# The first layer's condition weights in two pieces by output half, and a first feed-forward slot built up in two halves

## The reference, cut to what matters

```python
def _layer(x, c, l, prm, past):
    ada = jax.nn.silu(c) @ prm['w_ada'][l] + prm['b_ada'][l]
    ada = ada.reshape(B, N_SUB, 3, D)[:, :, :, None, :]

    def pre(j, z):
        return _rmsnorm(z, prm['g_pre'][l, j]) * (1 + ada[:, j, 1]) + ada[:, j, 0]

    def post(j, z, y, w):
        return (z + w * (1 + ada[:, j, 2]) * _rmsnorm(y, prm['g_post'][l, j])).astype(z.dtype)

    x = post(0, x, _swiglu(pre(0, x), prm['w_ffn_in'][l, 0], prm['w_ffn_down'][l, 0]), FFN_RES)
    y, st = _mix(pre(1, x), l, prm, past)
    x = post(1, x, y, 1.0)
    x = post(2, x, _swiglu(pre(2, x), prm['w_ffn_in'][l, 1], prm['w_ffn_down'][l, 1]), FFN_RES)
```

## Time and profile before

| | us |
|---|---|
| median of 3 runs | 1829.71 (1825.85 to 1831.72) |
| the profiled execution, its own time | 1823.39 |
| its span, first to last instruction | 1821.5 |
| mean granted TensorE clock in it | 0.978 of 2.4 GHz |
| PE busy | 1735.8 (95%) |
| DVE, ACT busy | 1053.0 (58%), 790.3 (43%) |

### The profile page before, as it was taken

The page is one execution under the profiler, slowest core; times in us unless marked ns, Lnnn a source line. Parts: engine busy times, 40 slices in busy tenths (PEclk is TensorE's granted clock), DMA queues, the critical chain, the costliest instruction groups (busy, mean ns, idle before and its releaser), DMA issues. The chain is left out here.

```text
span 1821.5 us, 33383 instructions
## 1 busy us (share of the span) xinstructions
PE 1735.8 (95%) x12724; PEld 1509.6 (83%) x12724; DVE 1053.0 (58%) x1903; ACT 790.3 (43%) x1428; POOL 67.2 (4%) x99
## 2 busy tenths in 40 slices
PE   5999999999998999999979999999999899989998
PEld 3898978878875687999969889788878667879997
DVE  3554555576567656565455554465665666665653
ACT  2554434345333215555345554344345222255552
POOL 0000000000000000000000000100000000000000
PEclk8999999999998999999999999999999989999999
DMA  8778555546448925555657784664553597355561
GB/s 335 266 268 329 212 219 199 208 163 242 164 164 278 318 93 203 182 174 209 253 195 278 265 336 163 231 242 152 193 203 139 196 329 256 116 203 173 179 220 58
DMA packets 85947, 391.83 MB, mean 215 GB/s; under 512 B 12472, under 2 KB 17856, under 8 KB 55488
## 3 DMA queue, kind: packets, MB, share of 16 engines
q1 hardware_dynamic: 72664, 368.15, 55.6%
q10 hardware_dynamic: 13160, 22.02, 3.4%
HBM read 377.31 MB, written 12.83 MB: 214 GB/s over the span
## 5 line engine op out<-in xcount | busy, mean ns | idle before, releaser
L1100 DVE TENSOR_TENSOR ring_parts<-ring,pages_parts 128x1024 fp32r<-128x1024 f32 (+1 forms) x288 | 334.0, 1193 | 157.6 <-ACT pages_parts L1716 157.5
L567 PE MATMUL ps<-arena_parts,pages_parts 128*128 128x264 f32 x1536 | 395.0, 291 | 18.0 <-DVE xn_parts L1188 10.4
L1716 ACT ACTIVATE pages_parts<-ring 128x1024 fp32r<-128x1024 f32 (+1 forms) x288 | 285.4, 1029 | 178.5 <-DMA ring<-in_w_ffn_in 55.3
L568 PE MATMUL ps<-xn_parts,pages_parts 128*128 128x264 f32 x1408 | 357.5, 288 | 0.0
L567 PEld LDWEIGHTS ps<-arena_parts,pages_parts 128*128 128x128 f32 x1536 | 295.1, 192 | 36.7 <-issue 30.2
L568 PEld LDWEIGHTS ps<-xn_parts,pages_parts 128*128 128x128 f32 x1408 | 269.2, 191 | 0.0
L572 PE MATMUL ps<-arena_parts,ring_parts 128*128 128x264 f32 x1536 | 222.8, 285 | 0.0
L528 PE MATMUL ps<-xn,ring 128*128 128x264 f32 x896 | 208.7, 388 | 0.3 <-ACT xn L1723 0.3
L572 PEld LDWEIGHTS ps<-arena_parts,ring_parts 128*128 128x128 f32 x1536 | 202.4, 190 | 0.0
L528 PEld LDWEIGHTS ps<-xn,ring 128*128 128x128 f32 x896 | 166.7, 190 | 33.8 <-ACT gates L1830 3.5
L567 PE MATMUL ps<-big_parts,pages_parts 128*128 128x264 f32 x704 | 176.0, 285 | 0.0
(11 more groups left out here) (351 smaller groups left out, 2556.5 us busy)
## 6 DMA issues: line engine op xcount, KB each, us to landing
ring<-in_w_ffn_in SPq DMA_DIRECT2D x88, 1024.0 KB, 5.0
ring<-in_w_ada SPq DMA_DIRECT2D x32, 1536.0 KB, 6.7
ring<-in_w_a SPq DMA_DIRECT2D x32, 1536.0 KB, 7.2
ring<-in_w_ffn_down SPq DMA_DIRECT2D x32, 1408.0 KB, 6.1
pages<-in_k_pages SPq DMA_DIRECT2D x128, 256.0 KB, 5.3
pages<-in_v_pages SPq DMA_DIRECT2D x128, 256.0 KB, 4.0
ring<-in_w_ada SPq DMA_DIRECT2D x24, 1024.0 KB, 6.6
ring<-in_w_proj SPq DMA_DIRECT2D x8, 1536.0 KB, 9.7
```

What stands on the lines that cost most here:

```text
L567: mm(ps[:, b, 0:T], tile, hi[:, k, :], start=start, stop=False)
L568: return mm(ps[:, b, 0:T], tile, lo[:, k, :], start=False, stop=False)
L1100: v.tensor_tensor(ring_lo[:, r, at * P:(at + n) * P], w, whi[:, place, 0:n * P].bitcast(F32), ALU.subtract)\
L1716: A(whi[:, place, 0:n * P], ring[:, r, at * P:(at + n) * P], ACT.Copy).then_inc(S.whi_ready, 1)
```

## The change

The eight loads of shift and scale weights become sixteen of half a megabyte. Piece `p` (0 or 1) holds, for both shift and scale, the columns of channel chunks 4p to 4p+3, over all input chunks. They don't go through the ring but into `big`, `gates`, `pj` and `wbuf`, which are free at that time, so that SP needs to wait for nothing: piece 0, then slot 0's feed-forward weights, then piece 1. Of each partition's row of a load, two runs of 512 numbers (2 KB) are read where it was one of 2048 (8 KB).

PE does piece 0, the first half of piece 1 (input chunks 0 to 3), then for chunks 0 to 3 all 24 products of slot 0 (`early_products`), the other half of piece 1, and the 24 products of chunks 4 to 7. DVE and ACT go through tables, modulation and split of the input by piece (`early_columns`, `early_split`); slot 0's weights are split on DVE between the two. Of the constants, only the identity and the ones are loaded at the start. The masks (into `pj`), the other four constants, `sel` and the page table are issued behind the fourth `w_ada12` load; the masks are made into bytes behind feed-forward slot 18. For the first layer the loops of two rounds are written out; the second layer keeps them.

```diff
@@ SP
-                    sp.dma_start(consts[:], ins.consts).then_inc(S.k_in, 16)
+                    sp.dma_start(consts[:, 0:2, :], ins.consts[:, 0:2, :]).then_inc(S.k_in, 16)
                 def late_loads():
-                    sp.dma_start(tt8, ins.masks).then_inc(S.t_in, 16)
+                    sp.dma_start(masks_in, ins.masks).then_inc(S.t_in, 16)
+                    sp.dma_start(consts[:, 2:6, :], ins.consts[:, 2:6, :]).then_inc(S.t_in, 16)
...
+                def load_early(p):
+                    for q in range(QUARTERS):
+                        for g in range(2):
+                            columns = ins.w_ada8[layer, g * QUARTERS + q].rearrange("p (u h c) -> p u h c", u=2, h=EARLY)
+                            sp.dma_start(early_block(p, g, q), columns[:, :, p, :]).then_inc(page_full[p * (1 + q // 2)], 16)
                 if first_layer:
-                    for k in range(8):
-                        load(ins.w_ada8[layer, k], 1)
-                        if k == 3:
-                            late_loads()
+                    load_early(0)
+                    load(ins.w_ffn_in[layer, 0, 0], 2)
+                    load_early(1)
+                    for k in range(16):
+                        if k:
+                            load(ins.w_ffn_in[layer, 0, k], 2)
+                        if k % 2:
+                            load(ins.w_ada12[layer, k // 2], 1)
+                        if k == 7:
+                            late_loads()
@@ PE
+                def early_ada(p, quarters):
+                    if quarters[0] == 0:
+                        adas()
+                        pe.wait_ge(S.ada_row, p + 1)
+                    home = p * (1 + quarters[0] // 2)
+                    pe.wait_ge(page_full[home], early_loads[home])
+                    for k in range(2 * quarters[0], 2 * quarters[-1] + 2):
+                        for j in range(4):
+                            g, c = divmod(j, 2)
+                            last = mm(ps[32 * j:32 * j + NB + 1, M0, 0:2 * P], csil[:, k, :],
+                                      early_block(p, g, k // 2)[:, k % 2, c * 2 * P:(c + 1) * 2 * P],
+                                      start=(k == 0), stop=(k == KC - 1))
+                    if quarters[-1] == QUARTERS - 1:
+                        last.then_inc(S.edone, 1)
+                        ada_columns(p, 8)
+                def early_products(p, r, homes):
+                    for b, place, m in homes:
+                        pe.wait_ge(S.wlo_ready, m + 1 + since(S.wlo_ready))
+                    for k in range(4 * p, 4 * p + 4):
+                        pe.wait_ge(S.xn_ready, k + 1 + since(S.xn_ready))
+                        for b, place, m in homes:
+                            last = upper(b, place, k, xhi, xlo, k == 0)
...
+                        for j, (b, place, m) in enumerate(homes):
+                            last = lower(b, r, j * KC + k, k, xhi, k == KC - 1)
...
+                    early_ada(0, range(4))
+                    early_ada(1, range(2))
+                    pe.wait_ge(S.evac, n + 1 + since(S.evac))
+                    early_products(0, r, homes)
+                    early_ada(1, range(2, 4))
+                    early_products(1, r, homes)
@@ DVE
-                    level_masks()
-                    for g in range(2):
-                        for _ in ada_rows(8):
-                            pass
-                        ada_columns(g, 8, g * 8)
...
-                    split_input(1, xhi, xlo)
-                    split(2 * KC)
+                    early_columns(0)
+                    early_split(0)
+                    split(2 * KC)
+                    early_columns(1)
+                    early_split(1)
+                    v.nop().then_inc(S.xsmp, 1)
                     lower_bounds()
@@ ACT
-                    modulate(1)
+                    for p in range(EARLY):
+                        act.wait_ge(S.esmp, p + 1)
+                        for c in range(4 * p, 4 * p + 4):
+                            act.wait_ge(S.xp_ready, c + 1)
+                            A(xn[:, c, 0:TP], xn[:, c, 0:TP], ACT.Identity, scale=atab[:, c, 0:1],
+                              bias=ada[:, c, 0:1]).then_inc(S.xmod, 1)
```

More of the change, by code:

```diff
@@ L596, in ffn_slot, with first_ffn_slot @@
                     ffn_products(open_slot(2))
[L598 removed]
+                def first_ffn_slot(before, slot=None):
                     r = open_slot(2) if slot is None else full(slot)
@@ new lines, in tensor @@
+                if first_layer:
+                    r, _, _ = slots.take(2)
+                    homes = []
+                    for _ in range(2):
+                        b, n = products.take()
+                        homes.append((b, *pieces.take()))
+                    early_ada(0, range(4))
[4 more added lines that the diff above has]
+                    early_products(1, r, homes)
@@ L1292, in vector @@
                             next(rows_of)
-                        if k == 7:
+                        if k % 8 == 7:
                             next(rows_of)
-                        ffn_slot(k, i * 8 + k, slot)
-                    ada_columns(i + ada0, 12, i * 12 + ADA_LOOP)
+                        ffn_slot(k, k, slot)
+                        if k % 8 == 7:
+                            ada_columns(ada0 + k // 8, 12, k // 8 * 12 + ADA_LOOP)
+                else:
+                    dve.wait_ge(S.ada_evac, 1 + since(S.ada_evac))
+                    scale_table(0)
+                    ahead.follow(slots)
+                    split(2 * KC)
+                    scale_shift_split(1)
+                    with dve.Fori(0, 2) as i, slots.loop(i, 2, [2, 2, 1] * 4), ahead.loop(i, 2, [2, 1, 2] * 4), \
+                            products.count.loop(i, 2, 16), pieces.count.loop(i, 2, 16), hids.loop(i, 2, 8), \
+                            exps.loop(i, 2, 8), link.loop(i, 2, 8):
+                        rows_of = ada_rows(12)
+                        for k in range(8):
+                            if k % 2:
+                                ahead.take(1)
+                            split(2 * KC)
+                            slot = slots.take(2)
+                            if k % 2:
+                                next(rows_of)
+                            if k == 7:
+                                next(rows_of)
+                            ffn_slot(k, i * 8 + k, slot)
+                        ada_columns(i + ada0, 12, i * 12 + ADA_LOOP)
                 rows_of = ada_rows(12)
@@ L1789, in scalar @@
                     start()
-                    for k in range(8):
-                        slots.take(1)
                     ahead.follow(slots)
@@ L1804, in scalar @@
                     shift_upper(1)
-                with act.Fori(0, 2) as i, slots.loop(i, 2, [2, 2, 1] * 4), ahead.loop(i, 2, [2, 1, 2] * 4), \
-                        products.count.loop(i, 2, 16), pieces.count.loop(i, 2, 16), exps.loop(i, 2, 8), \
-                        link.loop(i, 2, 16):
-                    for k in range(8):
+                if first_layer:
+                    for k in range(16):
                         if k % 2:
@@ L1811, in scalar @@
                         split(2 * KC)
-                        ffn_slot(k, i * 8 + k)
+                        ffn_slot(k, k)
                         if k % 2:
                             slots.take(1)
+                else:
+                    with act.Fori(0, 2) as i, slots.loop(i, 2, [2, 2, 1] * 4), ahead.loop(i, 2, [2, 1, 2] * 4), \
+                            products.count.loop(i, 2, 16), pieces.count.loop(i, 2, 16), exps.loop(i, 2, 8), \
+                            link.loop(i, 2, 16):
+                        for k in range(8):
+                            if k % 2:
+                                ahead.take(1)
+                            split(2 * KC)
+                            ffn_slot(k, i * 8 + k)
+                            if k % 2:
+                                slots.take(1)
                 for k in range(16, FC):
```

169 lines of the change are left out of this document (101 added, 68 removed).

## The result

The changed kernel takes 1830.62 us (median of 20 runs, 1826.16 to 1836.89) where the kernel before takes 1826.05 on the same chip (20 runs, 1816.73 to 1832.62): ratio 1.0027, 95% interval 1.0014 to 1.0040. It is slower by 2.6 to 7.3 us, centre 4.9. The forecast was +1.6 us, and 1831.3 on the median shown then. The difference is less than 0.3% (5.5 us) from no change, as forecast, on its slower side; its interval leaves no change out and reaches beyond the 0.3%. It lies above the forecast's own case (-0.5 to +4, chance 0.58) and inside the whole range. That 1831.3 and 1830.62 nearly agree is luck: the median of the kernel before was 1829.71 over 3 runs and is 1826.05 over 20, and this makes up for a change that was forecast too small.

A forecast was written before the change was run, and what follows sets the result against it. The kernel was taken as matmul-bound after the start, so slot 1's start decides: +1.4 us there and +0.2 for late loads give +1.6, 1825.0 on the profiled 1823.39 and 1831.3 on the median 1829.71; range 1824.5 to 1837.

The forecast's parts named there:

- Loads: Start: short rows stream at 404 GB/s; piece 0 lands at 18.0 us, last condition weights at 30.9 or 32.4.
- The rival of slow short rows: Start: 2 KB rows load at 299 GB/s, piece 0 lands 3.6 us later; +5.2 us, 1834.9; chance 0.09.
- the batch rule: Condition loads: transfers should be at least 1 MiB; sixteen of 0.5 MB lose 16 us, 1846; chance 0.02.
- Piece 0 on PE: Start, PE: four groups of condition matmuls, two low and two high clock, 5.9 us, done at 23.9.
- The split on the path: Start, DVE: slot 0's weights split behind the first half of the input, 2.37 us; first products at 31.7.
- It overlaps after all: Start: weights' split runs while piece 1 loads, products done by 31; -2.3 from the forecast, about 1829; chance 0.05.
- First 24 products: Start, PE: behind DVE's split from 31.7, 18 at low clock and 6 at high, 4.8 us, to 36.5.
- Last 24 products: Start, PE: behind the second tables from 42.7, 16 at low clock and 8 at high, 4.6 us, to 47.3.
- Slot 1: End of the start: slot 1 begins at 47.3 against 45.89, +1.4 us; its own weights' split just hidden.
- the rival of the low clock: Start: clock low on all bursts, products from 47.3 to 52.8; +6.9 us, 1836.8; chance 0.10.
- Late loads: Slot 8: four issues and 768 KB (1.9 us) precede its load; transposes wait 0.2 us, range 0 to 1.9.
- Sum: Whole kernel: +1.4 at slot 1 plus 0.2 for late loads, +1.6 us; 1831.3 on the median of runs.

The follow-up runs named there:

- the order experiment: Changed kernel with piece 1's last 16 condition records ahead of the first 24 products on PE; 1827.18 us, ratio to the kernel before 1.0008.
- DVE-order run: Changed kernel with the split of slot 0's weights ahead of piece 0's tables on DVE; 1826.72 us, ratio to the kernel before 1.0009.
- the repeated pair: Second profiles of both kernels, nothing changed: 1831.31 us (before) and 1835.64 us (changed).
- the combined one without a piece: Two runs: combined kernel without its six unread products (1826.12 us, ratio 1.0005), or with `lower_bounds` back ahead of slot 1's split (1823.78 us, 0.9991).
- the combined kernel: Changed kernel plus DVE's order, earlier late loads, piece 1's second half in quarters, six unread products, slot 1's split before `lower_bounds`; 1822.13 us, ratio to before 0.9959.
- the first four experiments: Changed kernel with PE's order swapped (1827.18 us), DVE's split moved (1826.72), 28 unread products (1827.84), or late loads behind slot 2's load (1831.00).

## Why the prediction was right, point by point

The verdict, the place and the order of the waits held; the added time at slot 1 and the late loads' were forecast too small, and the closeness of 1830.62 to 1831.3 is luck, as said above. By the steps of the prediction:

- *Loads.* Piece 0 landed at 18.44, forecast 18.0. The rate is the term that was off: 391 and 387 GB/s in 8 to 16 instead of 404. The first half of piece 1 landed at 26.36, forecast 25.7, and the last condition weights at 31.8 (the order experiment's row), within the forecast 30.9 to 32.4. The rival of slow short rows (299 GB/s) is ruled out, and the batch rule of the Trainium skill, "DMA: Bandwidth & Descriptors", section Bandwidth (at least 1 MiB a transfer), is not borne out where transfers are queued: sixteen of half a megabyte streamed at 387 to 391 GB/s. The fit that the prediction took from that page stands in its section on the anatomy of one DMA, for DMAs issued from GpSimd, and SP issues these.
- *Piece 0 on PE.* 6.6 us, forecast 5.9: three groups low rather than two. The same code gave 5.2 in another execution (18.22 to 23.44, with the late loads moved), so this term has a spread of 1.4 by itself.
- *Tables and modulation* to the end of the fourth chunk: 25.08 to 30.18, 5.1 us; forecast 5.4.
- *The split on the path.* DVE 30.18, first product 32.79, forecast 31.7 plus the 0.44 and 0.7 above. Held, and the DVE-order run confirms it: with the split moved, the first product comes at 28.09. What mending that order would bring was priced too low: the rival *It overlaps after all* had 2.3 us less than the forecast, and slot 1 came 5.8 us earlier, some 0.5 of it by the clock.
- *First 24 products.* 5.5 us (32.79 to 38.25), forecast 4.8; nearly all low. *Second half of piece 1* 2.0 and high, forecast 2.1. *Tables* 2.0, forecast 2.2. *First product behind ACT* 1.9, as forecast. *Last 24 products* 4.5, forecast 4.6: high for a microsecond, then low, then high at the end. The sign "a clock of 0.50 in most of 42 to 46" was not seen: it was 0.99 in 40 to 45, through the whole gap, and 0.50 from 45 to 48. That the 4.6 fits although the low stretch came later than thought is partly luck.
- *Slot 1.* 48.6 for 47.3. The 1.3 is the landing (0.4), piece 0's clock (0.7) and the first products' clock (0.7), less 0.5 of small gains at the tables. So the forecast's +1.4 was +2.7 and, in the repeated pair, +2.9: a quarter of the way to the rival of the low clock, which needed two of three bursts all low; one was nearly, and the two others in the greater part.
- *Late loads.* Forecast 0.2, measured 0.6 to 0.8 in the changed kernel (0.2 in DVE's order run). In the profiled execution the step that was off is the delay of slot 8's weights. ACT began it 5.15 us later (92.77 for 87.62) where slot 1 was 2.7 later, so the four issues and their bytes cost 2.4, not 1.9; the slack of 1.7 that the step assumed was right, since what is left is 0.7.
- *Sum.* +1.6 forecast; the two pairs of traces locate +3.5 and +3.4 up to slot 22. The ratio says 4.9 (2.6 to 7.3), which contains them. Whether the change costs anything beyond them isn't settled: behind slot 22 the ten executions of kernels with the change took 1638 us on average (1627.7 to 1647.6) and the two of the kernel before 1631.6 and 1639.4. The ratios hint at it. Four kernels with the change begin slot 1 earlier than the kernel before, by 2.8 (PE's order), 3.1 (DVE's), 3.6 and 4.0 (the combined one without a piece), which alone would give 0.9978 to 0.9984; they measured 1.0008, 1.0009, 1.0005 and 0.9991. Only the combined kernel lies on the other side. No run locates what is lost behind slot 1.

The prediction had named both places in the line, DVE's split and the first 24 products ahead of the last 16 records. What it hadn't seen is how much they cost: what stood between the two kernels was not the amount of work but who stands in line before whom. The chain of a piece runs over PE, DVE and ACT. Changing one order on PE gives back 5.6 us at slot 1, one on DVE 5.8 (5.3 without the clock's part). Both cost the change its gain in the same way: work that was ready stood behind work that wasn't.

That gain isn't seen in full in the medians: slot 1 came 5.6 and 5.8 us earlier than in the changed kernel, and the ratios went down by 0.0019 and 0.0018, 3.4 us. The intervals of the two ratios reach 3.4 and 4.7 us to either side, that of the changed kernel 2.4. That is compatible with 5.6 and doesn't show it.

## What to carry to other kernels

When a load is cut in pieces so that work can start early, follow for each engine its fixed order: whatever is ready sooner (here the weights' split) must stand ahead of the piece's chain, and the matmuls on which the next chain hangs ahead of those that only fill time. Work that was cut into bursts with waits between ran at the low clock for the greater part of each of the three bursts here; a few unread matmuls behind the last real ones before a known wait bought 1.4 us, but behind a wait of unknown length they delayed the real work. A gain of 5 us in the first 50 is lost from sight in 1800 unless it is measured at its place, and measured there it doesn't show that the whole gains as much.

## What the runs showed of the hardware

- **Issues slow down when the queue is full.** SP's queue in the changed kernel (start, length, count):

```profile
2.61 0.43 SPq L388 DMA_DIRECT2D lp<-in_layer_par  x1
...
3.82 4.63 SPq L423 DMA_DIRECT2D big<-in_w_ada  x7
...
17.73 1.18 SPq L423 DMA_DIRECT2D pj<-in_w_ada  x1
18.95 1.19 SPq L423 DMA_DIRECT2D gates<-in_w_ada  x1
```

  An issue takes 0.43 at first, 0.66 each in the first seven condition loads, and from the tenth load (9.79) on mostly 1.1 to 1.4, one of them 3.17. That is near the pace at which half a megabyte drains (0.5 MB at 387 GB/s is 1.35), from which it is inferred that a full queue holds the issues up. Slot 1's load was issued only at 21.41. It cost nothing here, since the engines stayed full; that a small urgent load behind such a row would wait is not shown.
- **Rows of 2 KB** drained at 387 to 391 GB/s in the changed kernel's full queue, of 4 KB at 402 to 411 (one execution, but for one slow stretch), of 8 KB at 419.
- **The clock's return varies from one execution to another.** The same matmuls from nearly the same start (18.22 and 18.44) got the full clock at 21.3 in one execution and at 24.4 in another, and slot 1 moved by 2.5 us. The Trainium skill, "TensorE: Matmul & The Clock Gate", Part 1, says that the throttled state is the default and activity releases it. The windows above agree with the second half, PE being busy when the clock rose, and add that the moment isn't fixed by the program. The first half isn't seen here: in the kernel before the profile gives 1.00 in 0 to 8 us, ahead of PE's first matmuls at 8.00.
- **The spread of executions goes with the clock.** Of the 31 executions of the kernel before that ran beside the first four experiments, the fastest two (1814.19 and 1814.40 us) had mean granted clocks of 0.985 and 0.983, the slowest two (1832.51 and 1831.98) 0.977 and 0.976; over all 31 the correlation of time and clock is -0.82.
